# Routing by two sorted lists, a gather for each expert, and a start without a meeting, in a two-layer RWKV-7 / MLA encoder on one core

## What is computed

```python
def expert_choice_ffn(h, w_router, w_gate, w_up, w_down):
    b, s, _ = h.shape
    cap = EC_CAPACITY * s // N_EXPERTS
    aff = jax.nn.softmax((h @ w_router).astype(jnp.float32), axis=-1)
    gates, idx = lax.top_k(jnp.swapaxes(aff, 1, 2), cap)
    b_idx = jnp.arange(b)[:, None, None]
    xe = h[b_idx, idx]
    hid = (jax.nn.silu(jnp.einsum('becd,edf->becf', xe, w_gate))
           * jnp.einsum('becd,edf->becf', xe, w_up))
    ye = jnp.einsum('becf,efd->becd', hid, w_down) * gates[..., None].astype(h.dtype)
    return jnp.zeros_like(h).at[b_idx, idx].add(ye)
...
        x = x + mix
        x = x + expert_choice_ffn(rms_norm(x, norm_ffn_g[i]), moe_router[i],
                                  moe_w_gate[i], moe_w_up[i], moe_w_down[i])
```

## Time and profile before

| | |
|---|---|
| Time, median of 3 runs | 1900.12 us (1898.45 to 1905.87) |
| The profiled execution's own time | 1901.98 us |
| Its span, to which all times of rows refer | 1900.2 us |
| TensorE busy | 1772.0 us, 93% |
| VectorE, ScalarE, GpSimd busy | 819.0, 559.6, 153.1 us |
| Mean granted clock of TensorE | 0.977 |
| Moved by DMA | 459.69 MB, mean 242 GB/s |

### The profile page before, as it was taken

How to read it: one execution, slowest core, us unless ns; L and a number is a source line. 1 busy time by engine, 2 the same in 40 slices (tenths; PEclk the granted TensorE clock), 3 DMA queues, 4 the chain that set the end, 5 groups by cost and what they waited for, 6 DMA issues and landing times.

```text
span 1900.2 us, 40296 instructions
## 1 busy us (share of the span) xinstructions
PE 1772.0 (93%) x17576; PEld 898.3 (47%) x17576; DVE 819.0 (43%) x1562; ACT 559.6 (29%) x1161; POOL 153.1 (8%) x230
## 2 busy tenths in 40 slices
PE   7999999999999599999988998999996999999998
PEld 4456666666555333333333355666543333333333
DVE  7867777776653412222211234777414222112212
ACT  3456555655542111111110123555320111101110
POOL 2101110111011100000000011111120000000000
PEclk9999999999999799999999998999997999999999
DMA  4101101110314999999999942000276999999998
GB/s 130 37 19 45 38 24 35 45 38 24 110 69 150 366 377 427 428 427 427 427 428 426 417 165 112 24 24 25 98 304 249 428 427 428 427 427 428 427 428 343
DMA packets 92184, 459.69 MB, mean 242 GB/s; under 512 B 16997, under 2 KB 50154, under 8 KB 68202
## 3 DMA queue, kind: packets, MB, share of 16 engines
q1 hardware_dynamic: 89994, 449.78, 58.5%
q0 software_dynamic: 2016, 7.34, 1.0%
HBM read 449.23 MB, written 7.86 MB: 241 GB/s over the span
## 4 chain that ended last, share of the span: by engine, by line
PE 73%; DMA 10%; issue 7%; DVE 3%; ACT 2%; SPq 2%; DVEq 1%; POOL 1%; POOLq 1%; another core or an unknown queue 1%; ACTq 0%; PEldq 0%
PE banks L1780 26%; PE banks L549 9%; DMA arena<-in_moe_w_down 7%; PE banks L1802 5%; PE banks L854 4%; PE banks L1433 4%; DMA arena<-in_moe_w_up 3%; PE banks L2355 3%; PE banks L2220 2%; PE banks L2380 1%; PE banks L2368 1%; PE banks L834 1%; PE banks L566 1%; SPq L1957 1%; PE banks L1748 1%
## 5 line engine op out<-in xcount | busy, mean ns | idle before, releaser
L1780 PE MATMUL banks<-arena 128*64 128x512 f32 x2944 | 657.4, 601 | 32.1 <-DMA arena<-in_moe_w_down 20.2
L1780 PEld LDWEIGHTS banks<-arena 128*64 128x64 f32 x2944 | 209.7, 138 | 442.7 <-issue 411.3
L1945 DVE TENSOR_TENSOR arena<-arena,banks 128x512 f32<-128x512 f32 x128 | 88.1, 688 | 285.1 <-PE banks L1802 285.1
L549 PE MATMUL banks<-arena 128*128 128x512 f32 x384 | 192.1, 618 | 0.0
L1885 ACT ACTIVATE arena<-banks 128x512 f32<-128x512 f32 x32 | 34.1, 1066 | 394.1 <-PE banks L1780 394.1
L1929 DVE SCALAR_TENSOR_TENSOR arena<-arena,banks 128x512 f32<-128x512 f32 x32 | 34.1, 1064 | 217.7 <-ACT arena L1885 217.7
L1802 PE MATMUL banks<-arena 128*128 128x512 f32 x256 | 114.7, 598 | 1.5 <-DVE arena L1942 1.5
L854 PEld LDWEIGHTS banks<-arena 64*64 64x64 f32 x5120 | 83.7, 134 | 62.9 <-issue 51.4
L1932 DVE SCALAR_TENSOR_TENSOR arena<-arena,small,banks 128x512 f32<-128x512 f32 x32 | 35.6, 1112 | 174.6 <-PE banks L1780 174.6
L854 PE MATMUL banks<-arena 64*64 64x64 f32 x5120 | 95.0, 221 | 2.6 <-issue 0.9
L549 PEld LDWEIGHTS banks<-arena 128*128 128x128 f32 x384 | 64.8, 189 | 51.5 <-issue 43.1
(11 more groups left out here) (307 smaller groups left out, 2217.7 us busy)
## 6 DMA issues: line engine op xcount, KB each, us to landing
arena<-in_moe_w_gate SPq DMA_DIRECT2D x64, 2048.0 KB, 32.5
arena<-in_moe_w_up SPq DMA_DIRECT2D x64, 2048.0 KB, 35.1
arena<-in_moe_w_down SPq DMA_DIRECT2D x54, 2048.0 KB, 36.2
arena<-in_moe_w_down SPq DMA_DIRECT2D x24, 512.0 KB, 11.6
arena<-in_moe_w_down SPq DMA_DIRECT2D x8, 1024.0 KB, 26.1
arena<-in_x SPq DMA_DIRECT2D x8, 512.0 KB, 7.5
arena<-in_rw_wr SPq DMA_DIRECT2D x8, 512.0 KB, 4.3
arena<-in_rw_wk SPq DMA_DIRECT2D x8, 512.0 KB, 4.2
```

The source lines that it names most:

```text
L549: last = nc.tensor.matmul(b[:, :], w_sl[:, n, k, :], xmix[n][:, k, :], start=(k == 0), stop=(k == ND - 1))
L1780: last = nc.tensor.matmul(b[z * CAP:(z + 1) * CAP, :], st[:, k, :], ring[g % RING][:, k, z * 512:(z + 1) * 512], start=(c % 2 == 0 and k = ...
L1945: nc.vector.tensor_tensor(xs, xs, b[:, :], ALU.add).then_inc(free[xj[("add", i, j)][0]], 1)
```

## The change

- **Start.** The masks stand ahead of and between the first norms on VectorE; GpSimd counts `consts_ready` up once more, after its first two index tiles. The gate's first weights have a semaphore count of their own.
- **No meeting.** The engines go from the start straight into the pairs; counters run on (`nth`, `rj` continues `pj`). Direction 0's products wait only for direction 0's operands, and in the first pair the sum of the gate's quarters and the turned values stand between the two directions. The gate's two scalings move into the pair on VectorE. Pair 1's weights are loaded as pair 0's are read.
- **Three slots.** Operand tiles of the pairs move into the ring's first three slots, which are free once the last pair's operands are used; SyncE loads chunks 0 to 2 of layer 0 in the last pair.
- **Two lists.** The first three tiles of tokens (384) are routed while the fourth is projected: softmax, transposes, and six of eight rounds. The fourth tile (128) has a list of its own. The two sorted lists of 64 are merged to each expert's 64th largest value and the number above it; comparisons give masks, and matmuls with triangular and all-one matrices give the places.
- **Gathers by expert.** The first pair's gather has four parts, width half z and expert e; expert 1's, and the columns for the row numbers and the transposes of `pick`, come after expert 0's gate projection.

The core of the diff:

```diff
+            for name in "rkv":
+                job_full(sp, pj, (name, 0))
+                projection_load(sp, name, 1)
...
+                if u == NPAIR - 1:
+                    sp.wait_ge(operands_ready, 2 * NPAIR)
+                    for g in range(PREPARED):
+                        job_full(sp, rj, ("U", 2 * g, 1, u))
+                        load_chunk(sp, 0, g)
...
-            for g in (0, 1, 2, 3, KEPT + 1, KEPT + 3) if layer == 0 else (0, 1, 2, 3, 4, KEPT + 1, KEPT + 3):
+            for g in (3, KEPT + 1, KEPT + 3) if layer == 0 else (0, 1, 2, 3, 4, KEPT + 1, KEPT + 3):
...
-                if u:
-                    pe.wait_ge(operands_ready, 2 * u)
+                pe.wait_ge(operands_ready, 2 * u + 1)
                 across(pe, "LR", Bt[0], 0, u)
+                if not u:
+                    gate_quarters_pe(pe)
+                    values_turned()
+                pe.wait_ge(operands_ready, 2 * u + 2)
                 across(pe, "LR", Bt[1], 1, u)
...
+            masks_dve(dve)
+            level_dve(dve, 0)
+            level_dve(dve, 1)
+            normed(0)
+            triangles_dve(dve)
+            level_dve(dve, 2)
+            normed(1)
+            level_dve(dve, 3)
+            normed(2)
             turned(0)
-            masks_dve(dve)
+            normed(3)
             turned(1)
...
+            def early_round(r):
+                top = early_top[0:NE, 8 * r:8 * r + 8]
+                nc.vector.max(top, early_work[0:NE, :])
+                dve.drain()
+                nc.vector.match_replace(early_work[0:NE, :], top, early_work[0:NE, :], -1.0)
+                dve.drain()
+
+            largest(0, NT - 1, "sel_early")
+            shares(0, NT - 1, "sel_early")
+            added(3, 0)
+            listed("at_early", early_work)
+            for r in range(3):
+                early_round(r)
+            added(3, 1)
+            early_round(3)
+            turned(3)
+            early_round(4)
+            largest(3, NT, "sel_late")
+            dve.sem_inc(hT_read[n], 1)
+            shares(3, NT, "sel_late")
+            early_round(5)
+            listed("at_late", late_work)
+            for r in range(CAP // 8):
+                nc.vector.max(late_top[0:NE, 8 * r:8 * r + 8], late_work[0:NE, :])
+                if r < 2:
+                    nc.vector.max(early_top[0:NE, 8 * r + 48:8 * r + 56], early_work[0:NE, :])
...
+            merged = late_work[0:NE, 0:CAP]
+            nc.vector.tensor_tensor(merged, early_top[0:NE, :], late_top[0:NE, ::-1], ALU.max)
+            dve.drain()
+            nc.vector.tensor_reduce(limit[0:NE, 0:1], merged, AX, ALU.min)
...
+            for i in range(2):
+                nc.tensor.matmul(rank[:, i, :, :], upto, above[:, i, :, :], start=(i == 0), stop=False, skip_group_check=True)
+                for t in range(NT - 1):
+                    later = NT - 1 - t
+                    last = nc.tensor.matmul(rank[:, i, t + 1:NT, :], every, above[:, i, t:t + 1, :].to_broadcast([P, later, NE]),
+                                            start=False, stop=(i == 1 and t == NT - 2), skip_group_check=True)
...
-        def gather_half_pe(pe, z, xj):
-            b = open_job(pe, xj, ("x", 0, z))
+            gather_half_pe(pe, 0, 0, xj)
+
+        def gather_half_pe(pe, z, e, xj):
+            b = open_job(pe, xj, ("x", 0, z, e))
             for t in range(NT):
                 for k in range(4):
-                    last = nc.tensor.matmul(b[:, k * P:(k + 1) * P], h_tok[:, t, (4 * z + k) * P:(4 * z + k + 1) * P], pick[:, t, :],
+                    last = nc.tensor.matmul(b[:, k * CAP:(k + 1) * CAP], h_tok[:, t, (4 * z + k) * P:(4 * z + k + 1) * P],
+                                            pick[:, t, e * CAP:(e + 1) * CAP],
...
                 up_to_hidden(("gate", i, 0), 0, 0)
+                if i == 0:
+                    for z in range(2):
+                        gather_half_pe(pe, z, 1, xj)
+                    rows_pe(pe, 0, layer)
+                    combination_pe(pe, 0, xj)
                 up_to_hidden(("up", i, 0), 0, 2)
```

More of the change, by code:

```diff
@@ L1480, in out_pe @@
                 turn_x(1)
-                out(3, 0)
+                out(3, 0, range(3))
                 logits(1)
                 turn_x(2)
-                out(3, 1)
-                logits(2)
             else:
@@ L1539, in out_act @@
                 scaled(1)
-                turned(2)
-                logits(2)
-                square(3)
             else:
                 square(0)
-                for t in range(1, NT):
+                for t in range(1, NT - 1):
                     turned(t - 1)
@@ L1991, in store_tokens @@
                 sp.dma_start(rows[:, t, :], h_tok[:, t, :]).then_inc(h_stored[layer], 16)
[L1993 removed]
+            for t in range(2 if layer == 0 else 3):
                 store_tokens(t)
@@ L1999, in load_experts @@
             load_chunk(sp, layer, KEPT)
-            store_tokens(NT - 1)
+            for t in range(2 if layer == 0 else 3, NT):
+                store_tokens(t)
             sp.wait_ge(routed[layer], 1)
```

347 lines of the change are left out of this document (206 added, 141 removed).

## The result

The changed kernel is slower: 1921.87 us against 1901.45, both medians of four runs; ratio 1.0103, 95% interval 1.009 to 1.0117. That is 20.4 us more, where 1901.4 was forecast and the range ended at 1911. The profiled execution has a span of 1920.8 (before 1900.2). One run of the ten of a later kernel (experiment 10, new start and two lists) took 6302.57 us where the other nine took 1894 to 1899, and it is left out of that kernel's median.

The account below looks back on a forecast made before the run. Each layer was taken to end a fixed weight stream after its first late refill. From the 1901.98 us profiled, -6.0 (start) and +7.3 (layers, +4.0 and +3.3) gave 1903.3, on the median 1901.4; range 1887 to 1911.

Parts of the forecast that it names:

- What bounds the kernel: Expert stages: a layer ends a fixed stream of weights after the first late refill, 19.1 and 19.8 us behind the gather's start.
- the stream: Expert weights arriving by DMA: restart equal to chunk 12 at 24.3 us behind the gather, against 19.1 and 19.8 before.
- first late refill: Expert stage's chunk 12, issued when the first gate projection ends and frees slot 1; forecast 16.1 us behind the gather's start.
- The start: Before and into the first pair: VectorE's wait gone, 2.2 us, and earlier operands, 3.8; 6.0 us gained, bounds 4 and 7.5.
- the rival in which the pairs take it up: RWKV pairs absorb the start's gain through a ScalarE and GpSimd chain that never waited for the operands; 1907.4 us, chance 0.10.
- Gathers by expert: Start of each expert stage: quarter gathers delay the weights by 5.2 us in layer 0 and 4.5 in layer 1.
- the hole: Expert weight loads: 13.1 us from chunk 12 until slot 2 is free for chunk 13, in which chunk 12 fills only 4.9.
- the second rival: Expert gathers: narrow ones cost half, chunk 12 at 12.5 and an equal stream from 17.3; 1887.4 us, chance 0.10.
- Three early chunks: Last RWKV pair: filling slots 0 to 2 before the pairs end gains nothing, since the first refill waits for TensorE either way.
- The two lists: Route from last projection to gather: gather 25.3 us behind the full early list; 1.2 us sooner in each layer.
- the rival of a route longer by 4: Route: early rounds on VectorE make it 4 us longer per layer instead of 1.2 shorter; 1911.8 us, chance 0.13.
- the hole is filled: Expert stages: the stream doesn't end a layer, so gains of 3.0 and 3.7 with 1.2 each stand; 1885 us, chance 0.08.

Follow-up runs that it names:

- experiment 10: First kernel: changed kernel without early loads, with the old half gathers, 1896.39 us, ratio 0.9975; second: kernel before with the new start alone, 1894.81 us, 0.9965.
- experiment 1: Changed kernel with two half gathers over 128 columns put back in place of four quarter gathers over 64; 1901.04 us, ratio to before 0.9996.
- experiment 8: Changed kernel without its three early loads, chunks 0 to 2 of layer 0 issued behind the last pair again; 1916.93 us, ratio 1.0098.
- experiment 7: Changed kernel with the second expert's gathers, row sums and combination moved behind half the first expert's up projection; 1923.13 us, ratio 1.0108.
- experiment 2: Changed kernel with its four quarter gathers each over 128 columns instead of 64, half of each result thrown away; 1912.67 us, ratio 1.0064.
- experiment 3: Changed kernel with unread 512-column matmuls added in each layer's route (3, 11 and 1) to keep TensorE at work; 1918.09 us, ratio 1.0082.
- experiment 5: Experiment 10's first kernel (new start, two lists, half gathers, no early loads) with experiment 3's added matmuls; 1893.08 us, ratio 0.9953.
- experiment 4: Experiment 11's kernel with the last 6 of its 17 wide added matmuls replaced by 24 of 64 columns; 1889.06 us, ratio 0.9933.
- experiment 6: Changed kernel with both quarter gathers over 128 columns and the added matmuls in the route (experiments 2 and 3 in one); 1909.42 us, ratio 1.0043.
- experiment 11: Kernel before with the new start and unread matmuls added in each layer's route (17 and 1); 1889.99 us, ratio 0.9946.

## Why the prediction was wrong, step by step

**The parts.** By the ratios, one step after the other: start -6.7, two lists +1.9 (not told from nothing), early loads +4.0 (experiment 1 against 10's first kernel), gathers +20.3 (the changed kernel against experiment 1). These four add up to the whole, 19.6, by construction. The forecast had +1.3, so it missed by some 18: 10.6 in the gathers (+20.3 for +9.7), 4.3 in the lists (+1.9 for -2.4), 4.0 in the early loads, and 0.7 the other way in the start. In another order, over experiment 8, gathers are +23.4 and early loads +1.0, but that kernel's interval is 14 us wide and tells nothing against the first order.

**What bounds the kernel: right.** Layers still end on weights, with 15 us of waits. The traces show more than that. Take as the stream's point the issue of chunk 12, or that of chunk 13 less 4.9 us where it is later (in experiment 7 chunk 15's less 14.7). In layer 1 this point lies anywhere between 1449.4 and 1485.2 in the fourteen traces, and the span ends 437.2 to 438.1 us behind it in every one. In layer 0 it lies between 665.6 and 688.6, and the gather of layer 1 comes 764.5 to 767.2 behind it. So what is lost or won ahead of the first late refill reaches the end one for one.

**The start: right.** -6.0 forecast, -5.98 on the row, -6.7 at the end by the ratio; the rival in which the pairs take it up falls. Some of the match is luck: as written, the terms 2.2 + 3.1 + 1 - 0.8 make 5.5 and not 6.0.

**Gathers by expert: the stream right, the first gather wrong.** This is the step that failed: "While the granted clock is at half, as it is in the wait before the gather, columns do cost, so the first quarter gather falls from 5.2 or 5.9 us to about 4.0". Columns don't cost at half clock either: the instructions start 0.213 us apart at both widths. The 5.2 and 5.9 were a gather that began at half clock and ended at full, and I read them as one of half clock throughout. The narrow one didn't bring the clock back, so all of it ran at half clock, and so did 2.7 us of the gate chunk behind it, for which the forecast had the full-clock 3.65. The forecast had the number in hand: for the rank it puts "slow-clocked up to 0.2 each".

Measured 7.09 for 4.0 and 5.0 for 3.65: 4.4 us of a stream 28.6 behind the gather where 24.3 was forecast. The rest of the step held: the full-clock quarter gather 3.79 (3.8), the hole 13.15 (13.1), and with the clock back inside the first gather (experiment 2) the stream is 25.6 and 26.0 behind. Gathers by expert were forecast at +9.7 in all; the rows give 18.0, of which 4.4 + 4.3 are the first gather's and gate chunk's at half clock, and the medians 20.8. Of what is left between rows and medians, 2.2 lie ahead of the layers and the last 0.6 is not placed.

The full-clock gathers also settle the second rival. Columns cost nothing there: 3.79 us for 32 instructions of 64 columns and 3.84 for 128, 0.12 each. The Trainium skill, TensorE: Matmul & The Clock Gate, section on LDWEIGHTS, with its P / 1.2 ns (107 ns at 128 weight columns), goes with these rows at full clock; at half clock they have 0.213, twice that. The Trainium skill's section Back-to-back issue gap, on the same page, gives about 60 cycles for a lone matmul of up to 64 columns and says itself that such figures leave out the weight load; they don't fit the rows here.

**Three early chunks, "nothing": wrong.** I asked only what they gain. What they collide with wasn't asked: with chunk 2 TensorE stands 2.15 us and has some clock less behind it, and the stretch is 3.7 longer.

**The two lists: late by more than the sum said.** The gather starts 28.7 behind the early list's copy, not 25.3. The late list's copy begins at A + 12.9 (1438.36 - 1425.43) where 11.7 was forecast, the limit's transposes stand at A + 22.4 (1447.88) for 20.6, so 1.8 is VectorE's; and the rank takes 3.6 where I took 2.0. I had its extra 1.4 in brackets ("slow-clocked up to 0.2 each, 1.4 more") and left it out of the sum, though TensorE waits 10.3 us ahead of it. At full clock the rank is 1.9 (experiments 3 and 5). So by experiment 10's rows the route got longer by 1.2 to 2.3 us and not shorter by 1.2; the rival of a route longer by 4 had the right sign and too large a size.

**The rivals and the range.** None was the result. That "the hole is filled" is refuted by experiments 1 and 7, and that narrow gathers cost half by the 3.79. The range ended at 1911 because no case held both half-clocked work and a price for the early loads.

## What to carry to other kernels

Where TensorE comes out of a wait (here of 10 to 16 us ahead of the rank and the gathers), cost its next matmuls at half clock, and don't read a row that began at half clock as one of half clock: see in the windows where the clock rises. Making the first matmuls narrower can make them slower and lengthen what follows; try both widths. Cutting an operation into pieces with the same stationary blocks doubles its weight loads, and where the ring of weights is full, each microsecond of that ahead of the first freed slots goes to the end, in both places tried here. A load into free slots isn't free either: look at what runs while it fills the DMA engines, and try it with one transfer fewer before giving it up.

## What wasn't expected of the hardware

- Matmuls that each load weights of 128 columns start 0.213 us apart at a clock of 0.50 and 0.112 at 1.00, with 64 moving columns as with 128.
- The granted clock stays at 0.50 through 7.09 us of back-to-back matmuls of 64 columns (ten of ten), and comes back inside those of 128 columns that began at 0.50 (twelve of twelve). At full clock, 5.5 us of 64-column matmuls didn't bring it down (experiment 4).
- It can fall to 0.50 while TensorE is at work (experiments 3 and 6, behind the rank, in both layers), and not do so in the same order of instructions elsewhere (experiment 5). Cause open.
- Where the third early load of 2 MB comes in, TensorE stands 1.9 to 2.4 us in the middle of queued matmuls, waiting for nothing that the profile shows (six of six), and it doesn't without that load (eight of eight).
- Matmuls that nobody reads, put into TensorE's waits of the route, made a kernel 4.8 us faster by the medians, 3.6 by the ratios (experiment 11 against start only).
